# First FFN steps round and split ahead of their sums, no zero matmuls in gate steps, own buffers for one last step, and the attention projection ahead of the gated unit

## The reference, cut to what matters

```python
# first block (one layer)
proj = u @ w_in; gates = sigmoid(u @ w_gate + b_gate)
y_ssm = gelu(ssm(u_ssm)); y_ssm = y_ssm * sigmoid(y_ssm @ w_glu + b_glu)      # the gated unit
y_attn = stick_breaking_attention(q, k, v)
merged = g_ssm * (y_ssm @ w_up_ssm) + g_attn * (y_attn @ w_up_attn)          # up projections
h = h + merged @ w_out
hid = relu(rmsnorm(h) @ w_ff1); h = h + (hid * hid) @ w_ff2                  # d_ff = 4096
# second block, two layers, each
x = LN(ALPHA * x + 0.5 * (silu(x @ wg) * (x @ wu)) @ wd)                     # "fa", d_ff = 2816
x = LN(ALPHA * x + token_mixer(x))                                           # "mix"
x = LN(ALPHA * x + 0.5 * (silu(x @ wg) * (x @ wu)) @ wd)                     # "fb"
```

## Time and profile before

| what | us |
|---|---|
| median of three runs | 1690.17 (1689.16 to 1690.76) |
| the profiled execution, its own time | 1691.35 |
| its span, first to last instruction | 1689.6 |
| PE (matmul) busy | 1627.6, 96% |
| DVE busy | 1110.5, 66% |
| ACT busy | 828.2, 49% |
| mean granted TensorE clock | 0.989 |

### The profile page before, as it was taken

The page is one execution under the profiler, slowest core; times in us unless marked ns, Lnnn a source line. Parts: engine busy times, 40 slices in busy tenths (PEclk is TensorE's granted clock), DMA queues, the critical chain, the costliest instruction groups (busy, mean ns, idle before and its releaser), DMA issues.

```text
span 1689.6 us, 24642 instructions
## 1 busy us (share of the span) xinstructions
PE 1627.6 (96%) x9690; PEld 1381.5 (82%) x9690; DVE 1110.5 (66%) x1480; ACT 828.2 (49%) x1077; POOL 49.7 (3%) x58
## 2 busy tenths in 40 slices
PE   6999899999999999999999999999999999999997
PEld 5876697888788888887888888788889877978886
DVE  5976766666766568865576655856577765665556
ACT  5455745343454346655454434634355655454443
POOL 1330100000000000000000000000000000000001
PEclk9998999999999999999999999999999999999999
DMA  7521343555655655532345556455664513454652
GB/s 205 159 66 51 100 142 122 196 179 194 215 174 174 199 199 149 176 101 75 125 150 174 183 189 209 166 172 186 211 193 132 175 51 100 150 173 154 205 188 100
DMA packets 206812, 264.53 MB, mean 157 GB/s; under 512 B 14106, under 2 KB 176276, under 8 KB 206740
## 3 DMA queue, kind: packets, MB, share of 16 engines
q1 hardware_dynamic: 206548, 263.50, 48.3%
q10 hardware_dynamic: 192, 0.04, 0.0%
HBM read 262.47 MB, written 1.05 MB: 156 GB/s over the span
## 4 chain that ended last, share of the span: by engine, by line
PE 86%; DVE 9%; ACT 2%; SPq 1%; issue 1%; DMA 0%; ACTq 0%; DVEq 0%
PE bank L445 41%; PE bank L484 21%; PE bank L486 11%; DVE wl L412 3%; PE bank L1612 2%; PE bank L1639 2%; PE bank L1205 1%; PE bank L1625 1%; ACT wh L405 1%; PE bank L679 1%; DVE wl L431 1%; PE bank L812 1%; DVE norm_small L731 1%; PE bank L1194 1%; PE bank L1640 1%
## 5 line engine op out<-in xcount | busy, mean ns | idle before, releaser
L484 PE MATMUL bank<-u_parts,wh 128*128 128x512 f32 x1664 | 590.6, 399 | 1.5 <-DVE u_parts L775 1.0
L412 DVE TENSOR_TENSOR wl<-raw,wh 128x2048 fp32r<-128x2048 f32 (+2 forms) x228 | 510.1, 2241 | 114.3 <-ACT wh L405 111.2
L405 ACT CAST wh<-raw 128x2048 fp32r<-128x2048 f32 (+3 forms) x235 | 437.2, 1864 | 89.5 <-PE bank L445 80.5
L486 PE MATMUL bank<-u_parts,wl 128*128 128x256 f32 x1664 | 467.0, 281 | 0.0
L484 PEld LDWEIGHTS bank<-u_parts,wh 128*128 128x128 f32 x1664 | 312.6, 188 | 79.4 <-issue 1.9
L486 PEld LDWEIGHTS bank<-u_parts,wl 128*128 128x128 f32 x1664 | 314.2, 189 | 1.9
L445 PE MATMUL bank<-u_parts,wh 128*128 128x256 f32 (+1 forms) x1344 | 257.3, 292 | 8.1 <-ACT tmp L1427 6.3
L445 PEld LDWEIGHTS bank<-u_parts,wh 128*128 128x128 f32 (+1 forms) x1344 | 212.0, 194 | 12.9 <-ACT tmp L1427 6.5
L445 PE MATMUL bank<-u_parts,wl 128*128 128x256 f32 (+1 forms) x672 | 192.0, 286 | 0.0
L445 PE MATMUL bank<-wh,hh 128*128 128x512 f32 x448 | 179.0, 400 | 6.6 <-DVE wl L412 4.5
L445 PE MATMUL bank<-wl,hh 128*128 128x512 f32 x448 | 174.7, 390 | 0.0
(11 more groups left out here) (340 smaller groups left out, 2036.2 us busy)
## 6 DMA issues: line engine op xcount, KB each, us to landing
raw<-ffn_wg SPq DMA_DIRECT2D x44, 1024.0 KB, 5.8
raw<-ffn_wu SPq DMA_DIRECT2D x44, 1024.0 KB, 5.3
raw<-ffn_wd SPq DMA_DIRECT2D x44, 1024.0 KB, 5.0
raw<-w_ff SPq DMA_DIRECT2D x32, 1024.0 KB, 5.3
raw<-w_in SPq DMA_DIRECT2D x28, 1024.0 KB, 5.6
raw<-w_out SPq DMA_DIRECT2D x12, 1024.0 KB, 5.0
raw<-w_gate SPq DMA_DIRECT2D x8, 1024.0 KB, 5.6
raw<-w_in SPq DMA_DIRECT2D x16, 512.0 KB, 5.4
```

The costliest lines, as they stand in the source:

```text
L405: ins = act.copy(dst, src)
L412: ins = dve.tensor_tensor(dst, src, upper.bitcast(F32), ALU.subtract)
L484: pe.matmul(two(bank[b + f]), slab_view(wh, slot, KD, WCOLS)[:, k, f * P:(f + 1) * P], u_parts[:, k, :, :], start=k == 0, stop=False, skip ...
L486: mm = pe.matmul(bank[b + f][:, 0:T], slab_view(wl, slot, KD, WCOLS)[:, k, f * P:(f + 1) * P], uh[:, k, :], start=False, stop=k == KD - 1, ...
```

## The change

- `ffn_split`: in the opening steps (gate(0), and up(0) in the second net) rounding and splitting slab n+2 stand ahead of the copy and the sum of slab n, on ScalarE and VectorE.
- `ffn_pe`: no `zero_banks` behind gate(0) in the five FFNs. `seed` for banks 0 to 3 waits for the norm's last tile instead, and the transposes of `big_pe` set the start flag on the first of four only.
- First net's FFN: the last hidden tile goes to `bh`, `bl` rather than `hh`, `hl`, and is formed right behind the last gate step's sum rather than behind the last but one down step.
- First net: TensorE's order is attention projection, gated unit, attention projection, SSM, SSM; the gated unit uses banks 2, 3. ScalarE's, VectorE's and the loads' order follow.

The diff, without two hunks that only drop arguments of `pe_up` and `dve_up` in the second net:

```diff
@@ -128,11 +128,13 @@
         add("gate1", n)
+    mark("up1")
+    add("up_attn", 0)
     mark("glu")
     add("glu", 0)
-    mark("up1")
-    for n, w in enumerate(("up_attn", "up_ssm", "up_attn", "up_ssm")):
-        add(w, n // 2)
+    add("up_attn", 1)
+    add("up_ssm", 0)
+    add("up_ssm", 1)
     mark("out1")
@@ -495,12 +497,11 @@
                 pe.wait_ge(hid_ready, i + ih0 + 1)
-                xh, xl = (bh, bl) if has_up and last else (hh, hl)
+                xh, xl = (bh, bl) if last else (hh, hl)
                 pe.wait_ge(seeded, j)
...
             gate(n0, ready=first_ready)
-            zero_banks(pe, 0)
             if has_up:
@@ -523,8 +524,11 @@
             def step(n, what, i, more=0, i0=0):
+                opening = isinstance(i, int) and i == 0 and what != "down"
+                if opening:
+                    do(eng, n + 2, more)
                 epilogue(what, n, i, more)
-                if n + 2 < len(slabs):
+                if n + 2 < len(slabs) and not opening:
                     do(eng, n + 2, more)
@@ -557,7 +561,10 @@
-            act.wait_ge(bank_zero, j)
+            if b0 == 4:
+                act.wait_ge(bank_zero, (j - 1) // 3 + 1)
+            else:
+                act.wait_ge(norm_out, KD * j)
             if j == 2:
@@ -602,13 +609,13 @@
                     dve.tensor_tensor(gate_z, gate_z, halves(4)[0], ALU.add).then_inc(gate_sum, 1)
-                    if has_up or not (isinstance(i, int) and i == 0):
+                    if has_up or not (isinstance(i, int) and i in (0, iters - 1)):
                         return
...
                     i = i + 1
-                    if isinstance(i, int) and i == iters:
+                    if isinstance(i, int) and i >= iters - 1:
                         return
@@ -624,7 +631,7 @@
                 dve.wait_ge(hid_step, 2 * i + (2 * ih0 + 1))
-                last = has_up and isinstance(i, int) and i == iters - 1
+                last = isinstance(i, int) and i == iters - 1
                 xh, xl = (bh[:, 0:2, :], bl[:, 0:2, :]) if last else (hh[:, :, :], hl[:, :, :])
@@ -676,8 +683,9 @@
                             pe.wait_ge(y_dve, j + 1)
-                    mm = pe.transpose(bank[TURN_BANKS[j][k // 4] + tt][:, (k % 4) * P:(k % 4 + 1) * P],
-                                      y_tok[:, tt, k * P:(k + 1) * P], ident[:, :])
+                    mm = pe.matmul(bank[TURN_BANKS[j][k // 4] + tt][:, (k % 4) * P:(k % 4 + 1) * P],
+                                   y_tok[:, tt, k * P:(k + 1) * P], ident[:, :], is_transpose=True, start=k % 4 == 0,
+                                   stop=True, skip_group_check=True)
                     if tt == 1 and k % 4 == 3:
@@ -1332,27 +1340,34 @@
+            upper = lambda off: ((lambda k: bh[:, off + k, :]), (lambda k: bl[:, off + k, :]))
+            pe.wait_ge(o_taken, 4)
+            pe.wait_ge(bu_free, ST)
+            lin_pe(pe, N_UP1, 0, None, KS, 512, 4, *upper(KS))
             pe.wait_ge(gelu_l, 1)
-            lin_pe(pe, N_GLU, 0, None, KS, DS, 4, lambda k: bh[:, k, :], lambda k: bl[:, k, :])
-            def free_banks():
-                for b in range(2):
-                    pe.wait_ge(lin_free[b], 8)
-                pe.wait_ge(w_exp, HEADS)
-            pe_up(pe, N_UP1, 0, lambda: pe.wait_ge(o_taken, 4), lambda: pe.wait_ge(glu_l, 1), free_banks, 1)
+            pe.wait_ge(w_exp, HEADS)
+            lin_pe(pe, N_GLU, 2, None, KS, DS, 4, *upper(0))
+            pe.wait_ge(pair_read, 1)
+            lin_pe(pe, N_UP1 + 2, 0, None, KS, 512, 4, *upper(KS))
+            for b in range(2):
+                pe.wait_ge(lin_free[b], 8)
+            zero_banks(pe, 4)
+            pe.wait_ge(glu_l, 1)
+            lin_pe(pe, N_UP1 + 3, 2, None, KS, 512, 4, *upper(0))
+            pe.wait_ge(pair_read, 2)
+            lin_pe(pe, N_UP1 + 4, 0, None, KS, 512, 4, *upper(0))
             pe_out(pe, N_OUT1, 0, 1)
...
-        def pe_up(pe, n0, r, ready_b, ready_a, free_banks, extra=0, order="BA"):
+        def pe_up(pe, n0, r, ready_b, ready_a, free_banks):
             for q in range(4):
-                p, which = q // 2, order[q % 2]
+                which = "AB"[q % 2]
                 off = KS if which == "B" else 0
                 (ready_b if which == "B" else ready_a)()
-                if q == 0 and extra:
-                    pe.wait_ge(glu_sig, 1)
                 if q == 2:
@@ -1376,25 +1391,32 @@
-        def dve_up(dve, n0, r, q, order="BA"):
-            link = lambda ins: chain(dve, dve_n, dve_chain, ins)
-            p, which = q // 2, order[q % 2]
-            wait_used(dve, n0 + q)
+        def dve_gate(dve, n, b, which, p, o):
+
+            wait_used(dve, n)
             g0 = (KD if which == "B" else 0) + 4 * p
-            o = merged[:, 4 * p:4 * p + 4, :] if q % 2 == 0 else gated
             for f in range(2):
...
                 ins = dve.scalar_tensor_tensor(out=o[:, 2 * f:2 * f + 2, :], in0=gates[:, g0 + 2 * f:g0 + 2 * f + 2, :], scalar=1.0,
-                                               in1=two(bank[2 * (q % 2) + f]), op0=ALU.add, op1=ALU.mult)
+                                               in1=two(bank[b + f]), op0=ALU.add, op1=ALU.mult)
             ins.then_inc(pair_read, 1)
+
+        def dve_merge(dve, r, p, read):
+
+            dve.wait_ge(pair_read, 4 * r + read)
+            two_tiles = [slice(4 * p + 2 * f, 4 * p + 2 * f + 2) for f in range(2)]
+            for f, k in enumerate(two_tiles):
+                dve.tensor_tensor(merged[:, k, :], merged[:, k, :], gated[:, 2 * f:2 * f + 2, :], ALU.add).then_inc(merged_sum, 1)
+            for f, k in enumerate(two_tiles):
+                dve.wait_ge(merged_h, 4 * r + 2 * p + f + 1)
+                dve.tensor_tensor(ul[:, k, :], merged[:, k, :], uh[:, k, :].bitcast(F32), ALU.subtract).then_inc(merged_l, 1)
+
+        def dve_up(dve, n0, r, q):
+
+            p = q // 2
+            dve_gate(dve, n0 + q, 2 * (q % 2), "AB"[q % 2], p, merged[:, 4 * p:4 * p + 4, :] if q % 2 == 0 else gated)
             if q % 2:
-                dve.wait_ge(pair_read, 4 * r + q + 1)
-                two_tiles = [slice(4 * p + 2 * f, 4 * p + 2 * f + 2) for f in range(2)]
-                for f, k in enumerate(two_tiles):
-                    dve.tensor_tensor(merged[:, k, :], merged[:, k, :], gated[:, 2 * f:2 * f + 2, :], ALU.add).then_inc(merged_sum, 1)
-                for f, k in enumerate(two_tiles):
-                    dve.wait_ge(merged_h, 4 * r + 2 * p + f + 1)
-                    dve.tensor_tensor(ul[:, k, :], merged[:, k, :], uh[:, k, :].bitcast(F32), ALU.subtract).then_inc(merged_l, 1)
+                dve_merge(dve, r, p, q + 1)
@@ -1446,19 +1468,21 @@
             act.copy(bh[:, 0:KS, :], us[:, :, :]).then_inc(gelu_h, 1)
-            act_round(act, N_GLU + 2)
+            act_round(act, N_UP1 + 2)
             wait_used(act, N_GLU)
             for f in range(KS):
-                ins = act.activation(gated[:, f, :], bank[f // 2][:, (f % 2) * T:(f % 2 + 1) * T], ACT.Sigmoid,
+                ins = act.activation(gated[:, f, :], bank[2 + f // 2][:, (f % 2) * T:(f % 2 + 1) * T], ACT.Sigmoid,
                                      bias=v1("b_glu")(f))
             ins.then_inc(glu_sig, 1)
+            act_round(act, N_UP1 + 3)
             act.wait_ge(glu_y, 1)
             act.copy(bh[:, 0:KS, :], us[:, :, :]).then_inc(glu_h, 1)
-            for q in range(4):
-                act_round(act, N_UP1 + q + 2)
-                if q == 2:
-                    seed(act, 1, 4, 2.0)
-                act_up(act, N_UP1, 0, q)
+            act_round(act, N_UP1 + 4)
+            seed(act, 1, 4, 2.0)
+            act_round(act, N_OUT1)
+            act_up(act, N_UP1, 0, 1)
+            act_round(act, N_OUT1 + 1)
+            act_up(act, N_UP1, 0, 3)
             for q in range(4):
@@ -1485,18 +1509,25 @@
             dve_o(dve, 3)
+            dve_split(dve, N_UP1 + 2)
+            for b in range(2):
+                dve.wait_ge(lin_free[b], 8)
             dve.wait_ge(gelu_h, 1)
             dve.tensor_tensor(bl[:, 0:KS, :], us[:, :, :], bh[:, 0:KS, :].bitcast(F32), ALU.subtract).then_inc(gelu_l, 1)
-            dve_split(dve, N_GLU + 2)
+            dve_gate(dve, N_UP1, 0, "B", 0, merged[:, 0:4, :])
             dve.wait_ge(glu_sig, 1)
             dve.tensor_tensor(us[:, :, :], us[:, :, :], gated, ALU.mult).then_inc(glu_y, 1)
+            dve_split(dve, N_UP1 + 3)
             dve.wait_ge(glu_h, 1)
             dve.tensor_tensor(bl[:, 0:KS, :], us[:, :, :], bh[:, 0:KS, :].bitcast(F32), ALU.subtract).then_inc(glu_l, 1)
-            for b in range(2):
-                dve.wait_ge(lin_free[b], 8)
-            for q in range(4):
-                dve_split(dve, N_UP1 + q + 2)
-                dve_up(dve, N_UP1, 0, q)
+            dve_split(dve, N_UP1 + 4)
+            dve_gate(dve, N_UP1 + 2, 0, "B", 1, merged[:, 4:8, :])
+            dve_split(dve, N_OUT1)
+            dve_gate(dve, N_UP1 + 3, 2, "A", 0, gated)
```

(8 more changed lines are left out.)

## The result

The changed kernel takes 1702.39 us (median of 4 runs, 1701.47 to 1703.09) against 1690.47 (1689.16 to 1691.27) for the kernel before on the same chip: ratio 1.0069, 95% interval 1.0057 to 1.0080. It is 11.9 us slower, 7.4 us above the predicted time and 1.9 us above the top of the range. The profiled execution has a span of 1699.7 us, before 1689.6.

A forecast was written before the change was run, and what follows sets the result against it. TensorE's matmuls bound the FFN loops, so only idle time at seams counts: -5.5 - 1.9 + 0.9 + 6.6 = +0.1, plus 4.7 for the clock, gave 1696.1 us profiled, 1695.0 median; range 1689.0 to 1700.5.

The forecast's parts named there:

- What bounds the kernel: FFN loops: TensorE's matmuls are the bound, busy 16.90 of 16.90 us, so a seam's delay passes on in full.
- the rival in which the loops absorb them: Second net's FFN loops have slack and absorb the openings' 6.6 us: -6.5, 1683.7 us; chance 0.11.
- Term 1: First net's gated unit and projections: the last projection starts at 232.2 instead of 237.7, a gain of 5.5 us.
- Term 2: End of the first net's FFN: own tiles let the last down step start at 445.2, a gain of 1.9 us.
- term 3: Opening of the first net's FFN: gate(0)'s sum waits behind the split, delaying gate(1), a loss of 0.9 us.
- Term 4: Openings of the second net's four FFNs: down(0) starts later by 1.95 + 3 x 1.55, a loss of 6.6 us.
- I expect one or two falls in the four openings, 1.5 x 3.1 = +4.7: Second net's openings: long TensorE waits halve the clock once or twice, 3.1 us each; 1693.4 to 1696.5, chance 0.48.
- three or four fall: Rival: the clock falls at three or four of the second net's openings, +9.3 or +12.4: 1699.6 to 1702.7; chance 0.16.
- the safe one: The idle 2.0 us of TensorE at 445.1, across which the clock stayed at 1.00; 2.4 and 2.6 us counted near it.
- the warning against idle gaps: Skill's rule that idle TensorE gaps halve the clock; taken at its word, all four openings fall, 1702.7 us.

The follow-up runs named there:

- second net's openings undone: Changed kernel with the opening steps of the second net's four FFNs back in the old order, the first net's still reordered; 1692.96 us, ratio 1.0008 to the kernel before.
- openings alone: Kernel before with only the reordered openings, the 8 zero matmuls behind gate(0) kept; 1706.62 us, ratio 1.0088 to the kernel before.
- input first: Changed kernel with no opening reordered and VectorE splitting the gated unit's input ahead of the weight slab; 1688.49 us, ratio 0.9989 to the kernel before.
- all undone: Changed kernel with no opening step reordered in either net; 1689.66 us, ratio 0.9994 to the kernel before.

## Why the prediction was wrong

**What bounds the kernel** held: delays at the openings went through in full (ledger), and the rival in which the loops absorb them fell.

**Terms 1 to 4** held. Term 1: the seam ahead of the unit, the unit in 6.03 us and the last two projections from 224.94. With the 1.5 us by which this execution was early, that is the forecast 213.5 and 226.4. The chain that ended last shows them:

```profile
210.74 1.23 DVE bl L1516
211.97 0.04 issue
212.01 6.03 PE bank L447 x48
...
221.45 2.29 DVE wl L414
223.75 1.15 DVE bl L1522
224.89 0.04 issue
224.94 20.19 PE bank L447 x133
```

It gained 5.3 with clock where 5.5 was forecast. Term 2 gained 1.96 locally (predicted 1.9), term 3 lost 0.9 (0.9). Term 4 lost 2.1 + 1.2 + 1.4 + 1.2 = 5.9 (6.6); by "second net's openings undone" 6.2. The terms together were some 1.6 us too high, of which 0.7 is term 4 and 0.8 is outside the change (first and last line of the ledger).

**The step that failed** is "I expect one or two falls in the four openings, 1.5 x 3.1 = +4.7". There were six falls, in three kinds of place:
- In the openings of the second net three, not one or two: 3.95 us of idle time and more fell each time, and the one of 3.10 did not. The price was 3.0, 2.8 and 1.7: 7.5 together. The rival "three or four fall", at 1699.6 to 1702.7, had their number right. That its top, four times 3.1, is near the measured time is in part chance: these three cost less, and three others stood elsewhere. That all three long ones fell could have been expected from the trace before: it has three gaps of over 4 us, 4.35 at 98.0, 4.35 at 131.3 and 5.44 at 204.1, and the clock fell behind each. The prediction counted one instance.
- Behind the 2.36 us of the first net's gate(1), which the prediction had called near the safe one: 1.7.
- At 702.8 and 1327.4, places that the diff does not touch: 1.7 each. Just ahead of each stand 8 matmuls of 32x32, identical before and after. Timeline of PE, the kernel after:

```profile
699.48 3.79 PE L1757 MATMUL bank<-sq,tables 32*32 32x512 f32 x8
```

and the same in the kernel before, where no fall followed:

```profile
703.92 3.62 PE L1726 MATMUL bank<-sq,tables 32*32 32x512 f32 x8
```

Removing one fall at the gated unit, at 2.4, was counted. Six at 12.6 in place of it make +10.2, where the sum had 4.7 - 2.4 = +2.3. That is 7.9 too low; the terms' work without the clock was 1.6 too high, and the early start took 1.1 more: 7.9 - 1.6 - 1.1 = 5.2 for this execution, 1701.47 - 1696.1 = 5.4. The median misses by 2.0 more, because the execution profiled before lay 1.2 above its median and the one profiled after lies 0.9 below its own.

Counted over the twelve traces, the start-up of the weights (before 60 us) left out:

| gap between matmul starts, us | gaps | clock fell |
|---|---|---|
| 1.2 to 2.3 | 106 | 0 |
| 2.41 to 2.73 | 16 | 9 |
| 2.86 to 3.07 | 10 | 9 |
| 3.26 to 3.45 | 4 | 2 |
| 4.03 to 4.43 | 30 | 30 |
| 5.44 | 3 | 3 |
| none, behind the eight 32x32 matmuls | 24 | 13 |

The prediction held the 2.0 us idle wait at 445.1 to be safe and put 2.4 and 2.6 beside it. One fall in "openings alone" stands behind that very wait, gap 2.41, which did not fall before. So a middle length has no yes or no; it has odds. The same gap of 2.52 us ahead of the gated unit fell in four kernels and not in three, and of three gaps of 2.90 in "input first" two fell. What differs there is the moment at which it comes; that the moment decides is inferred from this and from the 32x32 matmuls, and no run shifted a gap in time on purpose. The executions of one kernel differ in the same way: the twelve of "all undone" spread over 6.6 us, and their granted clock goes with it, 0.989 at 1687.12 and 0.984 to 0.985 at the three above 1692. Those 0.005 of a span of 1690 us are worth up to 8 us. So the spread goes with the clock; where in the slow ones it fell no trace shows.

Of the Trainium skill (TensorE: Matmul & The Clock Gate, "Why this matters for your kernels") the warning against idle gaps was the better guide here. The traces agree for every gap from 4.0 us, and for 20 of the 30 between 2.4 and 3.5.

## What to carry to other kernels

Work moved ahead on an engine must be able to start there. Two things kept it from doing so here: the slot that TensorE still read (gate(0)'s follower, a net of 1.2 us), and, the larger one, the seeds ahead of it in ScalarE's queue (down(0)'s slab, whose slot was free all along, 5.2 us). In both cases what stood behind was put in line. The same slab rounded ahead of gate(0)'s copy fills idle time and gains. Look up who frees the slot, and what stands ahead in the queue, before reordering. When PE is the bound, price each gap from the length at which the traces show falls (here 2.4 us) with a chance of a fall, and compare two kernels with the half-clock time taken out of both, from a point behind the start-up. Matmuls with zeros that gain nothing in work may be what keeps a gap short.

## What the runs showed of the hardware

- Stretches at half clock, all but the last of each program, were 3.4, 6.8 or 10.2 us long. A fall that starts ahead of PE's return costs less, since part of it is idle: at 893.9 PE was busy in 6.00 of 6.80 us.
- The clock fell behind eight matmuls of 32x32 on 512 columns (3.6 us where the clock held), though PE reads as busy throughout: 3.40 of 3.40 us in the window at 699.4, with PEclk 1.00 in it and 0.50 in the next. It happened at 13 of 24 places, in none of the two before. The busy share does not show this; the PEld column does, 0.76 us there.
- The 4.35 us gaps at 98 and 131 us, alike in all kernels, were followed by stretches of 6.8 in some and 10.2 us in others: up to 1.7 us of difference in loss that has nothing to do with the edit.
